# Multiplying four chunks of the latent output before the norm behind the second dense layer is known

## The reference, cut to what matters

```python
# end of first_block, layer 1
f = squared_relu_mlp(rms_norm(h, ffn_pre_g[1]), w_ff1[1], w_ff2[1])
h = h + rms_norm(f, ffn_post_g[1])
# start of second_block, layer 0 (x is h)
h = rmsnorm(x, attn_norm[0])
proj = h @ w_in_even[0]
fq, fk, fv, ff, dq, ckv, dkr, iq, ik, iw = jnp.split(proj, split_points, axis=-1)
```

## Time and profile before

| what | us |
|---|---|
| median of three runs (1148.2 to 1148.44) | 1148.35 |
| the profiled execution | 1148.74 |
| its span, first to last instruction | 1146.8 |
| PE busy in the span | 1132.8 |
| DVE busy | 829.3 |
| ACT busy | 655.1 |
| POOL busy | 130.8 |

### The profile page before, as it was taken

The page is one execution under the profiler, slowest core; times in us unless marked ns, Lnnn a source line. Parts: engine busy times, 40 slices in busy tenths (PEclk is TensorE's granted clock), DMA queues, the critical chain, the costliest instruction groups (busy, mean ns, idle before and its releaser), DMA issues.

```text
span 1146.8 us, 26297 instructions
## 1 busy us (share of the span) xinstructions
PE 1132.8 (99%) x10447; PEld 963.3 (84%) x10447; DVE 829.3 (72%) x1345; ACT 655.1 (57%) x1026; POOL 130.8 (11%) x168
## 2 busy tenths in 40 slices
PE   9999999999999999999999999999999999999998
PEld 7768888888888888888877788888878678888887
DVE  7787976655777986655769869876666666978664
ACT  7665666434567576433575767564455666755432
POOL 0000200000203200000243310000125431000010
PEclk9999999999999999999999999999999999999999
DMA  8762475555563375565353437654674444665461
GB/s 343 263 203 75 129 239 197 196 187 191 174 231 108 113 257 188 180 218 193 139 184 111 153 142 234 207 168 144 201 254 150 133 147 149 236 207 173 152 186 52
DMA packets 31469, 206.60 MB, mean 180 GB/s; under 512 B 3488, under 2 KB 3872, under 8 KB 10144
## 3 DMA queue, kind: packets, MB, share of 16 engines
q1 hardware_dynamic: 31104, 205.00, 52.7%
q10 hardware_dynamic: 288, 0.52, 0.1%
HBM read 204.46 MB, written 1.05 MB: 179 GB/s over the span
## 4 chain that ended last, share of the span: by engine, by line
PE 91%; DVE 6%; ACT 1%; issue 1%; DVEq 0%
PE ps L642 21%; PE ps L643 21%; PE ps L644 21%; PE ps L997 1%; PE ps L905 1%; PE ps L907 1%; PE ps L906 1%; PE ps L1518 1%; PE ps L1520 1%; PE ps L1519 1%; PE ps L893 1%; PE ps L865 1%; PE ps L881 1%; PE ps L766 1%; DVE m L2454 1%
## 5 line engine op out<-in xcount | busy, mean ns | idle before, releaser
L1601 ACT ACTIVATE w_hi<-staged 128x2048 f16<-128x2048 f32 (+3 forms) x191 | 338.2, 1786 | 232.1 <-PE ps L644 222.0
L2394 DVE SCALAR_TENSOR_TENSOR w_lo<-staged,w_hi 128x2048 f16<-128x2048 f32 (+3 forms) x191 | 406.5, 2141 | 26.4 <-ACT w_hi L1601 26.1
L644 PE MATMUL ps<-f_hi,w_lo 128*128 128x256 f16 x1524 | 415.4, 273 | 0.0
L642 PE MATMUL ps<-f_hi,w_hi 128*128 128x256 f16 x1524 | 415.4, 273 | 0.0
L643 PE MATMUL ps<-f_lo,w_hi 128*128 128x256 f16 x1524 | 415.4, 273 | 0.0
L642 PE MATMUL ps<-x_hi,w_hi 128*128 128x256 f16 x672 | 183.3, 273 | 0.0
L643 PE MATMUL ps<-x_lo,w_hi 128*128 128x256 f16 x672 | 183.2, 273 | 0.0
L644 PE MATMUL ps<-x_hi,w_lo 128*128 128x256 f16 x672 | 183.2, 273 | 0.0
L643 PEld LDWEIGHTS ps<-f_lo,w_hi 128*128 128x128 f16 x1524 | 149.1, 98 | 18.1
L642 PEld LDWEIGHTS ps<-f_hi,w_hi 128*128 128x128 f16 x1524 | 149.2, 98 | 17.6 <-issue 0.2
L644 PEld LDWEIGHTS ps<-f_hi,w_lo 128*128 128x128 f16 x1524 | 149.1, 98 | 17.2
(11 more groups left out here) (398 smaller groups left out, 1876.9 us busy)
## 6 DMA issues: line engine op xcount, KB each, us to landing
staged<-weights SPq DMA_DIRECT2D x165, 1024.0 KB, 5.2
staged<-weights SPq DMA_DIRECT2D x32, 704.0 KB, 4.3
xn<-bands SPq DMA_DIRECT2D x3, 512.0 KB, 9.8
m<-bands SPq DMA_DIRECT2D x3, 512.0 KB, 8.1
cst<-constants SPq DMA_DIRECT2D x1, 1027.0 KB, 8.0
h<-x_turned SPq DMA_DIRECT2D x2, 512.0 KB, 4.7
staged<-weights SPq DMA_DIRECT2D x2, 512.0 KB, 6.8
qT<-bands SPq DMA_DIRECT2D x2, 512.0 KB, 11.6
```

What stands on the lines that cost most here:

```text
L642: pe.matmul(out, wh, xh[:, c, :], start=(c == 0), stop=False)
L644: last = pe.matmul(out, wl, xh[:, c, :], start=False, stop=(c == kc - 1))
L1601: act.activation(w_hi[:, s, o:o + n], staged[:, s, o:o + n], ACT.Copy, scale=SW).then_inc(hi_split, 1)
L2394: dve.scalar_tensor_tensor(w_lo[:, s, o:o + n], staged[:, s, o:o + n], SW, w_hi[:, s, o:o + n], ALU.mult, ALU.subtract).then_inc(lo_split, 1)
```

## The change

Output 3 (`ckv`) is no longer one `chunk(3)` behind `together`. Its first four chunk products (`PARTED = 4`) are made while the norm is being worked out, from what is there by then: the old residual `h * g_attn` (PSUM bank 3) and the unscaled output `m * g_post * g_attn` (bank 4), each split into high and low in the memory of `xn` by ACT and DVE during `ff2_1` (`part(c)`, one chunk in each of four units). The other four chunk products of output 3 run in `together` as a fourth output for `c >= 4`. DVE then joins: bank 4 times a copy of the token scale (`row_scale`, copied by ACT) plus bank 3, into `CKV`. The fills of this seam go. `chunk(3)` goes, `swap_index(0)` moves behind `chunk(4)`, output 4 is put into bank 6. ACT makes the high part of even half 4 ahead of its three evictions; DVE makes the join and even halves 3 and 4 ahead of its tables. Some semaphores are merged, and `both_gains` is one product of 128 x 4 at the start. The lines of the diff that only declare or rename semaphores are left out.

```diff
+PARTED = 4
@@ views
+        part_rows = xn[:].rearrange("p c t -> p (c t)").bitcast(F16).rearrange("p (k c t) -> p k c t", k=4, c=PARTED)
+        old_hi, old_lo, new_hi, new_lo = (part_rows[:, i] for i in range(4))
+        row_scale = stat[:, 1, :]
@@ TensorE
         def even_bank(n):
-            return n if n < 4 else 1 if n == 20 else n % 2
+            return n if n < 4 else 6 if n == 4 else 1 if n == 20 else n % 2
@@ together
-                    for j in range(n):
+                    for j in range(n + (c >= parted)):
@@
+            def parts(bank, xh, xl, first, end):
+
+                u = FIRST["even"]
+                for c in range(first, end):
+                    wh, wl = weights(u % 2, (3 * DC + c) * P, P)
+                    pe.matmul(ps[:, bank, 0:T], wh, xh[:, c, :], start=(c == 0), stop=False)
+                    pe.matmul(ps[:, bank, 0:T], wh, xl[:, c, :], start=False, stop=False)
+                    pe.matmul(ps[:, bank, 0:T], wl, xh[:, c, :], start=False, stop=(bank == 4 and c == PARTED - 1))
@@ sums
+                    if name == "ffn_post_1":
+                        arrived(2 * FIRST["even"] + 1)
+                        pe.wait_ge(part_lo, 2 * PARTED)
+                        parts(3, old_hi, old_lo, 0, 2)
                     pe.wait_ge(last_squared, BY_TOKEN.index(name) + 1)
...
-                    fill(5, 4)
+                    if name == "ffn_post_1":
+                        parts(3, old_hi, old_lo, 2, PARTED)
+                    else:
+                        fill(5, 4)
                     pe.wait_ge(inverted, i + 1)
...
                     last.then_inc(scale_rows, 1)
+                    if name == "ffn_post_1":
+                        parts(4, new_hi, new_lo, 0, PARTED)
...
-                keep_warm(4)
+                if layer == 0:
+                    keep_warm(4)
@@
-            together("even", 3, x_hi, x_lo, "attn_0")
-            chunk(3, 0, 3 * D)
+            together("even", 3, x_hi, x_lo, "attn_0", parted=PARTED)
+            chunk(4, 1, 0)
             swap_index(0)
-            chunk(4, 1, 0)
             columns("attn_0")
@@ ScalarE
+                def part(c):
+
+                    act.activation(old_hi[:, c, :], h[:, c, :], ACT.Copy, scale=v("attn_0", c)).then_inc(part_hi, 1)
+                    act.wait_ge(drained[two], c + 3)
+                    act.activation(new_hi[:, c, :], m[:, c, :], ACT.Copy, scale=both_gains[:, c:c + 1]).then_inc(part_hi, 1)
@@
+            act.wait_ge(scale_rows, POSTS.index("ffn_post_1") + 1)
+            act.activation(row_scale, TOKEN_SCALE, ACT.Copy).then_inc(part_hi, 1)
             last_halves("ff2_1", 1)
             root("attn_0")
@@
+            even_split(2, 4)
             for n in range(3):
                 even_evict(n, m[:, n, :])
-            even_split(2, 4)
-            even_evict(3, CKV)
             even_split(4, 5)
@@ VectorE
+                def part(c):
+
+                    dve.wait_ge(part_hi, 2 * c + 1)
+                    dve.scalar_tensor_tensor(old_lo[:, c, :], h[:, c, :], v("attn_0", c), old_hi[:, c, :], ALU.mult,
+                                             ALU.subtract).then_inc(part_lo, 1)
+                    dve.wait_ge(part_hi, 2 * c + 2)
+                    dve.wait_ge(drained[two], c + 3)
+                    dve.scalar_tensor_tensor(new_lo[:, c, :], m[:, c, :], both_gains[:, c:c + 1], new_hi[:, c, :], ALU.mult,
+                                             ALU.subtract).then_inc(part_lo, 1)
@@
             invert("attn_0")
+            dve.wait_ge(product["even"], 4)
+            dve.wait_ge(part_hi, 2 * PARTED + 1)
+            chain(dve.tensor_tensor(tmp[:, 2, :], ps[:, 4, 0:T], row_scale, ALU.mult))
+            dve.wait_ge(drained["even"], 3)
+            dve.tensor_tensor(CKV, ps[:, even_bank(3), 0:T], tmp[:, 2, :], ALU.add).then_inc(drained["even"], 1)
+            u0 = FIRST["even"]
+            split(2 * u0 + 3)
+            split(2 * u0 + 4)
             dve.wait_ge(inverted, NORM_AT["attn_0"] + 1)
             late_tables(2)
-            u0 = FIRST["even"]
@@
-            even_split(3, 4)
             rope_index(0)
             even_split(5)
```

More of the change, by code:

```diff
@@ L337, in conformer_mla_fox_dsa_moba_kernel @@
         latents = sb("latents", [P, 20])
+        both_gains = sb("both_gains", [P, PARTED])
         rope_keys = sb("rope_keys", [P, 2, T])
@@ L375, in conformer_mla_fox_dsa_moba_kernel @@
         h_first = sem("h_first")
+        part_hi = sem("part_hi")
+        part_lo = sem("part_lo")
         x_loaded = sem("x_loaded")
@@ L657, in part, with together @@
                         last.then_inc(product[name], 1)
-            def together(name, n, xh, xl, norm, squares=True):
+            def together(name, n, xh, xl, norm, squares=True, parted=DC):
                 arrived(2 * FIRST[name] + (n - 1) // 2)
@@ L1183, in _ @@
                     pe.wait_ge(rooted, NORM_AT["kv_norm"])
-                    pe.wait_ge(eps_terms, len(LATENT))
+                    pe.wait_ge(latent_terms, len(LATENT))
                     latent_sums("kv_norm")
@@ L1202, in _ @@
                     pe.wait_ge(latent_row_copied, 1)
-                    pe.wait_ge(key_scaled, 1)
+                    pe.wait_ge(latent_terms, len(LATENT) + 2)
                     latent_sums("q_norm")
@@ L1257, in even_free @@
             def even_free(n):
-                if n >= 4:
+                if n > 4:
                     pe.wait_ge(drained["even"], even_drained(n))
@@ L1913, in unit @@
                         hi(g, g // 2 % 2, i * 16 + 16 * (g // 4 + 1))
-                with act.Fori(0, units // 2 - 1) as i:
+                def part(c):
+                    act.activation(old_hi[:, c, :], h[:, c, :], ACT.Copy, scale=v("attn_0", c)).then_inc(part_hi, 1)
+                    act.wait_ge(drained[two], c + 3)
+                    act.activation(new_hi[:, c, :], m[:, c, :], ACT.Copy, scale=both_gains[:, c:c + 1]).then_inc(part_hi, 1)
+                looped = 1 if layer else units // 2 - 1
+                with act.Fori(0, looped) as i:
                     unit(i, 0)
                     unit(i, 1)
+                if layer:
+                    act.wait_ge(gains_scaled, 3)
+                for n in range(2 * looped, units - 2):
+                    unit(n // 2, n % 2)
+                    part(n - 2)
                 if layer == 0:
@@ L2041, in _ @@
                 act.activation(ROPE_ROWS[at], ps[at, even_bank(4), 0:T], ACT.Copy)
+            act.wait_ge(drained["even"], 4)
             act.activation(GATE_ROWS, ps[32:64, even_bank(4), 0:T], ACT.Copy).then_inc(drained["even"], 1)
@@ L2671, in _ @@
             dve.wait_ge(gains_scaled, 2)
+            dve.tensor_tensor(both_gains[:], v("ffn_post_1", 0, PARTED), v("attn_0", 0, PARTED), ALU.mult).then_inc(gains_scaled, 1)
             invert("mix_pre_0")
@@ L2810, in mlp @@
                 last = dict(STREAM)[two] // 2 - 1
-                with dve.Fori(0, last) as i:
+                def part(c):
[6 more added lines that the diff above has]
+                                             ALU.subtract).then_inc(part_lo, 1)
+                looped = 1 if layer else last
+                with dve.Fori(0, looped) as i:
                     unit(i, 0)
                     unit(i, 1)
+                for n in range(2 * looped, 2 * last):
+                    unit(n // 2, n % 2)
+                    part(n - 2)
                 unit(last, 0, layer == 1, True)
@@ L2829, in _ @@
                 dve.tensor_scalar(latents[:, 4 + 2 * e:6 + 2 * e], latent_cells(0), n * P * RMS_EPS / D, n * P * RMS_EPS ** 2, ALU.mult,
-                                  ALU.add).then_inc(eps_terms, 1)
+                                  ALU.add).then_inc(latent_terms, 1)
             def variance(name, dst):
                 e = LATENT.index(name)
-                dve.wait_ge(eps_terms, e + 1)
+                dve.wait_ge(latent_terms, e + 1)
                 dve.wait_ge(summed, NORM_AT[name] + 1)
                 dve.tensor_tensor(latents[:, dst:dst + 2], latent_cells(1 + e), latents[:, 4 + 2 * e:6 + 2 * e], ALU.add).then_inc(
-                    latent_variance, 1)
+                    latent_terms, 1)
             variance("kv_norm", 8)
```

8 lines of the change are left out of this document (3 added, 5 removed).

## The result

| | before | after |
|---|---|---|
| median, 11 runs each (us) | 1148.28 (1148.08 to 1148.79) | 1151.13 (1150.84 to 1151.72) |
| profiled execution / its span (us) | 1148.74 / 1146.8 | 1151.0 / 1149.1 |
| busy in the span: PE, DVE, ACT, POOL (us) | 1132.8, 829.3, 655.1, 130.8 | 1131.3, 834.2, 657.9, 132.0 |

The ratio is 1.0024, 95% interval 1.0016 to 1.0032. The change costs **2.85 us**. The forecast was +1.6, 1149.95, with a range up to 1151.1, which is given to a tenth: the median lies at its upper end, 0.03 us beyond. The sign and the place were as forecast; the size was not.

A forecast was written before the change was run, and what follows sets the result against it. PE was taken to bound nearly every stretch, so its shift at `index_dots(0)` was the program's: +0.44 + 1.20 - 2.62 + 0.2 + 1.9 + 0.55 = +1.65, taken as +1.6, 1149.95 us. Range 1147.6 to 1151.1.

The forecast's parts named there:

- part 5: Rope steps behind `chunk(5)`, with DVE's tables, half 5 and gates and POOL's cosine: adds 0.55 us, `index_dots(0)` at +1.65.
- Part 1: High and low parts made on ACT and DVE during `ff2_1`: cost nothing, covered by DVE's 4.07 us idle before each output.
- Part 2: Gap between the first sum and `together`: six matmuls delay the second sum and the row, so `together` starts +0.44 us.
- Part 3: `together` and `chunk(3)`: twelve more matmuls, +1.20 us net, and `chunk(3)` gone, -2.62; together -1.42.
- Part 4: Weights of `chunk(5)`: even half 4 comes late behind evictions and join; PE stalls +1.9 us, `chunk(5)` starts +1.1.
- POOL takes the port first: Slower rival: POOL's scaling starts before DVE's half 4, which waits 0.73 us; +2.3 us, up to +3.0; chance 0.17.
- three signs of being wrong: `w_lo` starting by 574.5, `together` ending before 572.0, or the DVE stretch from 597 coming out shorter than before.
- No stall: Faster rival: half 4 is ready when PE reaches `chunk(5)`; -0.8 us with the 0.2 wait, 1147.55; chance 0.12.
- The clock falls: Slower rival: PE's 1.9 us stall lowers its clock over `chunk(5)`, whose 24 matmuls cost 2.6 more; +4.2 us; chance 0.05.

The follow-up runs named there:

- e2: Changed kernel with the low parts of even halves 3 and 4 moved ahead of the second join operation: 1150.56 us, ratio 1.0015.
- e10: Changed kernel with DVE order reciprocal, tables, halves 3 and 4, joins, rope step 0, half 5, rope step 1, gates; POOL's cosine before scaling: 1147.76 us.
- e5: Changed kernel with POOL's cosine step of the first rope row put ahead of its scaling of CKV: 1150.58 us, ratio 1.0019.
- e9: Changed kernel with the second rope step ahead of the two gate operations in DVE's list: 1150.27 us, ratio 1.0016.
- e1: Changed kernel with the two late tables moved ahead of the join in DVE's list: 1150.63 us, ratio 1.0018.
- e3: Changed kernel with both the moves of e1 and e2, tables first and half 4 ahead of the second join operation: 1150.57 us, ratio 1.0016.
- e6: e3 with POOL's cosine step also put ahead of its scaling of CKV: 1149.17 us, ratio 1.0007.
- e12: Kernel before, without the change, with its second rope step ahead of the two gate operations: 1148.26 us, ratio 0.9998.
- e11: e10 with the first six partial matmuls moved from between the two sums to behind the second: 1147.62 us, ratio 0.9992.

## Why the prediction was off in size

The mechanism was right up to `chunk(5)`; the term that failed is the 0.55 us of part 5, the rope steps, which measured 1.99.

All times from the first sum; "forecast" are the prediction's shifts. Its +1.1 at `chunk(5)` counts from a row of the loads (576.89); from the matmul, at 577.00, it would be 1.0.

| step | before | after | shift | forecast |
|---|---|---|---|---|
| first high part of the residual | 3.52 | 3.80 | +0.28 | +0.44 |
| last low group of `together` | 14.22 | 15.58 | +1.36 | +1.53 |
| `chunk(5)` | 20.87 | 21.58 | +0.71 | +1.1 |
| `swap_index(1)` | 23.49 | 25.39 | +1.90 | +1.3 |
| `index_dots(0)` | 27.97 | 30.67 | +2.70 | +1.65 |

**Part 1** (parts in `ff2_1`) held: DVE still idles ahead of each output, 3.25 us where it was 4.07, and the two new operations take 0.48 us each:

```profile
541.25 0.48 DVE L2854 SCALAR_TENSOR_TENSOR xn<-h,vec,xn 128x256 f16<-128x256 f32 x1
541.64 0.48 DVE L2858 SCALAR_TENSOR_TENSOR xn<-m,both_gains,xn 128x256 f16<-128x256 f32 x1
545.37 0.43 DVE L2842 TENSOR_SCALAR m<-ps 128x256 f32<-128x256 f32 x1 [3.25 <-PE ps L651]
```

**Part 2** (the gap) held in kind; the term was 0.44 and measured 0.28, and the loads pause 0.61 us ahead of `together` where they paused 0.31. The first parts' loads begin 0.37 us after those of the first sum, not 0.53, so the 0.53 that is listed for a group is not what the next load has to wait:

```profile
555.54 0.53 PEld L743 LDWEIGHTS ps<-cst,stat 128*128 128x128 f32 x4
555.91 0.18 PEld L718 LDWEIGHTS ps<-xn,w_hi 128*128 128x128 f16 x1
...
556.56 0.53 PEld L750 LDWEIGHTS ps<-cst,sq 128*128 128x128 f32 x4
```

**Part 3** (work moved and saved) held: `together` grew by 1.36 - 0.28 = 1.08 up to its last low group, where 1.09 was due.

**Part 4** (the weights of `chunk(5)`) held: DVE's join waits for ACT's third eviction, half 4 starts right behind it, the wait is 1.45 us where 1.9 was expected. Half 4 ended at 21.5, where the forecast has 577.95 - 556.13 = 21.8: 0.16 of that is part 2, the rest small savings on DVE. The 0.2 us that the sum has for a wait of `swap_index(0)` is not listed as one: `swap_index(0)` starts 0.26 us behind the last matmul of `chunk(4)`, 0.15 more than the usual 0.11. e2 and e10 show the cause: with half 4 ahead of the join the wait is 0.16 and 0.28.

**Part 5** (the rope steps) is the step that failed in size. It was to add 0.55 between `chunk(5)` and `index_dots(0)` and added 1.99. Three prices were too low, by 0.51, 0.37 and 0.55 us, which is 1.43 of the 1.44:

- *The tables*, 0.8 us, took 1.31 from 577.09 to 578.40, because POOL's scaling, held back by half 4, came free just as half 4 ended. e5 takes this away (0.79 there).
- *L2948 behind the cosine step.* Before, it started 0.11 us behind POOL's recorded end, in after 0.48. With the cosine step that is 0.4 us more than the sum had.
- *The gate operations*, "two gate operations of 0.64 us each". These were never DVE's own times. The trace of before already said so: the first, at 581.39, ended at 582.03, and this POOL operation ended at 582.00:

```profile
580.73 1.27 POOL L2320 TENSOR_TENSOR m<-m,tmp 128x512 f32<-128x512 f32 x1 [3.21 <-PE ps L1306]
```

In after POOL's second cosine begins while DVE makes half 5 and is held until that ends, at about 583.05; the gate is then held until the cosine ends, and the two gates take 1.85 us (583.01 to 584.86) for the forecast's 1.3. e9 gives the price without POOL, 0.16.

So of the rivals, *POOL takes the port first* had the right mechanism in the wrong place. It was asked whether POOL would get in ahead of half 4. It did not: half 4 was first, as before. But then POOL's scaling is held for as long as half 4 runs, and takes its turn from whatever DVE has next, which stands on the same path. That the measured +2.85 lies in the +2.3 to +3.0 of that rival is luck in part: its 0.7 us at half 4 did not come, and other hold-ups took the place. *No stall* fell with the 1.45 us. *The clock falls* fell: the clock is 1.00 in every stretch of the seam, with waits of 1.45 and 1.02 us close together. The spacing of the matmuls says it more firmly than the granted clock does: at the start of the program, where the prediction puts the clock at 1.2 GHz from the durations of L766, the view of before has 1.00 as well, while thirteen matmuls of L766 from 2.55 on take 5.70 us, about 0.4 each, and the eight at 558.48 take 1.89, about 0.2 each. At the seam the spacing stays at 0.11.

None of the three signs of being wrong came: half 4 and the one column ahead of it start at 574.82, `together` ends at 571.66 (572.14 on the clock of before), and the stretch in which DVE decides is not shorter.

The Trainium skill ("SBUF — State Buffer", section "SBUF: two separate sides") has the lock taken, on DVE's side, also by operations with two inputs from SBUF, against a POOL operation that reads SBUF. The trace agrees, down to which operations pay: the table, the gates and L2948 have two such inputs and are held (0.95 for 0.42, 1.25 for 0.16, 1.14 for 0.69). The first operation of a rope step (L2883 in before, L2944 in after) reads one of its inputs from `ps` and is not held. In before it takes its usual 0.68 while POOL's scaling, let go by the end of half 4, runs to 576.29:

```profile
575.63 0.68 DVE L2883 TENSOR_TENSOR tmp<-ps,tmp 128x512 f32<-128x512 f32 x1
```

**What stays open:** why L2948 starts 0.48 us behind POOL's recorded end in the first rope step of the changed kernel, and 0.48 or 0.49 in e1, e2, e3, e5, e6 and e9, but 0.11 in before and in the second step of e9, 0.10 in both steps of e12. POOL's recorded spans are rough, and no run was made for it. It is 0.37 us of the 2.70, and in e10 and e11, where the operation starts 0.43 and 0.41 behind POOL's recorded end but right behind its own predecessor, it no longer costs PE anything that the trace shows.

## What to carry to other kernels

When work is taken off the engine that seems to bind, list what the other engines must deliver in the time that is now shorter, in their own order, and move the deliveries up together: single moves here brought 0.2 to 0.95 us each, the whole set turned +2.70 into -0.70. Before taking a DVE operation's duration from a trace, see whether a POOL operation ended at the same moment; if so, the duration may be that engine's, as with the gates here, and it will change when either list moves. A releaser beside the loads' idle time need not be a wait that costs: look whether the matmuls idle too.

## What was not expected of the hardware

- A DVE operation on 128 x 16 numbers took 0.16 us with POOL at rest, and 0.64 to 1.25 us beside a POOL operation: up to eight times its own time, and what it took beyond 0.16 was POOL's.
- An operation of POOL that was held back did not only lose time itself: it ran when DVE's long operation ended, and the next DVE operation paid 0.53 us (the table in after, 0.95, against 0.42 in e5).
- PE stood still for 1.45 us and again for 1.02 within the next 4 us and kept a granted clock of 1.00.
